# A two-layer mixer stack: square roots behind the last exponentials of differential attention, token differences beside the norm, a rearranged start and moved weight splits

## What is computed

```python
# A two-layer mixer stack: square roots behind the last exponentials of differential attention, token differences beside the norm, a rearranged start and moved weight splits
x = x + rmsnorm(nsa_mixer(rmsnorm(x, norm_pre[0]), ...), norm_post[0])
x = x + rmsnorm(diff_mixer(rmsnorm(x, norm_pre[1]), ...), norm_post[1])
# A two-layer mixer stack: square roots behind the last exponentials of differential attention, token differences beside the norm, a rearranged start and moved weight splits
p = softmax(q @ k.T + bias)                # two maps
o = (p[0] - lam * p[1]) @ v
o = rmsnorm(o, subln) * (1 - lambda_init)  # over the head's 128 columns
y = (o * silu(z)) @ w_out
# A two-layer mixer stack: square roots behind the last exponentials of differential attention, token differences beside the norm, a rearranged start and moved weight splits
xx = shift(u) - u                          # difference to the token before; -u for the first
xw = u + xx * mu[1]                        # and so on for k, v, a, g, r
```

## Time and profile before

| | |
|---|---|
| median of 3 runs | 2272.48 us (2271.74 to 2279.61) |
| the profiled execution, its own time | 2274.92 us |
| its span, first to last instruction | 2273.0 us |
| PE busy | 2070.1 us, 91% |
| DVE, ACT, POOL busy | 848.5, 935.9, 915.2 us |
| mean granted TensorE clock | 0.937 |

### The profile page before, as it was taken

One profiled execution on the slowest core, in us unless ns is written; L12 is line 12 of the kernel. 1 busy time (PEld: TensorE's weight loads), 2 busy tenths in 40 slices (PEclk: granted clock), 3 DMA queues, 4 the chain that ended last, 5 costly groups with the idle time before them and its releaser, 6 DMA issues.

```text
span 2273.0 us, 33586 instructions
## 1 busy us (share of the span) xinstructions
PE 2070.1 (91%) x13582; PEld 1661.5 (73%) x13582; DVE 848.5 (37%) x1813; ACT 935.9 (41%) x1707; POOL 915.2 (40%) x636
## 2 busy tenths in 40 slices
PE   4999999999997968997588899999999899999998
PEld 3889756788765746776477588888878568888886
DVE  2100467340027375146565353333033524334301
ACT  3431477453247354443133353444143535344422
POOL 2431267534446322341012734455434542544542
PEclk9987999999998969898589999999999999999999
DMA  4322100123310211221210323333322121333332
GB/s 119 93 78 65 47 20 2 48 69 101 93 56 19 70 42 49 76 75 38 49 31 19 101 62 98 102 93 111 102 75 84 38 66 56 102 97 98 103 111 74
DMA packets 222361, 161.05 MB, mean 71 GB/s; under 512 B 30631, under 2 KB 205295, under 8 KB 222208
## 3 DMA queue, kind: packets, MB, share of 16 engines
q1 hardware_dynamic: 220016, 151.83, 22.6%
q0 software_dynamic: 2192, 7.07, 1.0%
HBM read 153.64 MB, written 5.24 MB: 70 GB/s over the span
## 4 chain that ended last, share of the span: by engine, by line
PE 79%; DVE 9%; ACT 4%; POOL 3%; issue 3%; DMA 1%; POOLq 1%; SPq 0%; DVEq 0%; PEld 0%; PEldq 0%; ACTq 0%
PE ps L386 15%; PE ps L348 13%; PE ps L350 13%; PE ps L359 13%; PE ps L396 7%; PE ps L1355 2%; PE ps L1368 2%; PE ps L1344 2%; POOL weights_lo L289 1%; DVE ps L901 1%; DVE buffer L906 1%; PE ps L1082 1%; PE ps L2892 1%; PE ps L2156 1%; PE ps L1703 1%
## 5 line engine op out<-in xcount | busy, mean ns | idle before, releaser
L289 POOL TENSOR_TENSOR weights_lo<-buffer,weights_hi 128x1024 fp32r<-128x1024 f32 (+1 forms) x265 | 654.0, 2470 | 981.4 <-ACT weights_hi L278 981.2
L278 ACT ACTIVATE weights_hi<-buffer 128x1024 fp32r<-128x1024 f32 (+1 forms) x265 | 276.4, 1045 | 340.7 <-PE ps L396 285.5
L348 PE MATMUL ps<-u_hi,weights_hi 128*128 128x512 f32 (+1 forms) x752 | 278.5, 378 | 5.6 <-DVE u_lo L681 3.0
L350 PE MATMUL ps<-u_lo,weights_hi 128*128 128x512 f32 (+1 forms) x736 | 274.8, 377 | 0.0
L1931 ACT ACTIVATE buffer<-ps,buffer 128x512 f32<-128x512 f32 x88 | 68.7, 781 | 276.4 <-PE ps L359 276.4
L359 PE MATMUL ps<-u_hi,weights_lo 128*128 128x512 f32 (+1 forms) x752 | 177.2, 378 | 0.0
L1961 DVE SCALAR_TENSOR_TENSOR buffer<-ps,buffer,buffer 128x511 f32<-128x511 f32 x88 | 66.0, 750 | 287.7 <-ACT buffer L1931 287.7
L348 PEld LDWEIGHTS ps<-u_hi,weights_hi 128*128 128x128 f32 x752 | 141.2, 190 | 32.0 <-issue 5.6
L350 PEld LDWEIGHTS ps<-u_lo,weights_hi 128*128 128x128 f32 x736 | 138.4, 188 | 25.5
L359 PEld LDWEIGHTS ps<-u_hi,weights_lo 128*128 128x128 f32 x752 | 137.0, 191 | 25.8
L2932 ACT ACTIVATE buffer<-ps 32x256 f32<-32x256 f32 (+5 forms) x96 | 47.7, 498 | 152.9 <-PE ps L2892 68.1
(11 more groups left out here) (403 smaller groups left out, 4277.5 us busy)
## 6 DMA issues: line engine op xcount, KB each, us to landing
buffer<-in_w_up SPq DMA_DIRECT2D x88, 512.0 KB, 3.8
buffer<-in_w_down SPq DMA_DIRECT2D x44, 512.0 KB, 3.4
buffer<-in_diff_w_in SPq DMA_DIRECT2D x32, 512.0 KB, 4.0
buffer<-in_nsa_w_in SPq DMA_DIRECT2D x28, 512.0 KB, 3.8
buffer<-in_w_rkv SPq DMA_DIRECT2D x24, 512.0 KB, 4.1
buffer<-in_nsa_w_out SPq DMA_DIRECT2D x8, 512.0 KB, 3.5
buffer<-in_diff_w_out SPq DMA_DIRECT2D x8, 512.0 KB, 3.6
buffer<-in_w_o_rwkv SPq DMA_DIRECT2D x8, 512.0 KB, 3.4
```

The costliest lines, as they stand in the source:

```text
L278: self.nc.scalar.activation(self.part_hi[:, part % self.PARTS, 0:n], self.raw[:, ld % self.RAW, 0:n], ACT.Copy).then_inc(self.hi_ready, 1)
L289: self.nc.gpsimd.tensor_tensor(self.part_lo[:, part % self.PARTS, 0:n], self.raw[:, ld % self.RAW, 0:n], self.part_hi[:, part % self.PARTS ...
L348: nc.tensor.matmul(out, hi[:, k, :], rhs[0][:, k, tokens], start=(k == 0), stop=False)
L350: nc.tensor.matmul(out, hi[:, k, :], rhs[1][:, k, tokens], start=False, stop=False)
```

## The change

1. Start: x comes as three transfers; the barriers after `Setup` and `Norm` are gone on all engines; the small vectors and the bias table's source are fetched after the first three weight tiles, and their turns and copies stand in `NsaProject` before the bias table; the norm's scaling is one DVE operation (`Renorm.scale`) instead of one on DVE and one on ACT; ACT loads its Sqrt table first.
2. `DiffAttend`: the first root now covers batches 0 to 5 and stands after the last exponentials, the others one batch each behind it; all norms stand after the last unit, in the order 0, 2, 4, 6, 1, 3, 5, 7; all engines go on to `Output` without a barrier, whose turns wait for the count of norms (`wait_rows`).
3. `Output` before `RwkvProject`: DVE makes the differences by token tile (`difference`) between the steps of the norm, the last one at the head of `RwkvProject`; ACT's order of squares, units, high parts and splits is another.
4. `SwaProject` and `SwaAttend`: of the three splits in the loop, one now stands at the end of the projection, two after the loop.
5. `FfnUp`: both layers share one set of semaphores; the order on each engine is the same. The diff is cut to its added and removed lines; this edit, `Setup`'s memory, and `FfnUp`'s lines are left out.

```diff
@@ -525,8 +527,14 @@
     def load(self, sp):
...
-        sp.dma_start(env.x, io["x"].rearrange("b (t p) d -> p (b t) d", p=P)).then_inc(self.x_arrived, 16)
-        sp.dma_start(env.const, io["shape_constants"]).then_inc(self.const_arrived, 16)
+        for i, end in enumerate((1, 2, NT)):
+            sp.dma_start(env.x[:, i:end, :],
+                         io["x"][0, i * P:end * P, :].rearrange("(t p) d -> p t d", p=P)).then_inc(self.x_arrived[i], 16)
+            if i == 0:
+                sp.dma_start(env.const, io["shape_constants"]).then_inc(self.const_arrived, 16)
...
+    def load_vectors(self, sp):
+        io = self.env.io
@@ -549,23 +557,23 @@
-    def tensor(self, pe):
+    def vectors_tensor(self, pe):
...
-        pe.wait_ge(self.const_arrived, 16)
-        pe.wait_ge(self.tab_arrived, 64)
...
-            tr = nc.tensor.transpose(env.ps[:, n // 4, (n % 4) * P:(n % 4) * P + size], self.rows[0:size, n, :],
+            tr = nc.tensor.transpose(env.ps[:, 6 + n // 4, (n % 4) * P:(n % 4) * P + size], self.rows[0:size, n, :],
...
     def bias_tensor(self, pe):
...
+        pe.wait_ge(self.tab_arrived, 64)
+        pe.wait_ge(self.table_ready, 1)
...
-            if i >= 4:
-                pe.wait_ge(self.bias_taken, i - 3)
+            if i >= 2:
+                pe.wait_ge(self.bias_taken, max(i - 2, 1))
@@ -573,12 +581,14 @@
     def vector(self, dve, step):
-        env, nc = self.env, self.env.nc
-        nc.vector.memset(env.eps, EPS)
+        nc = self.env.nc
+        nc.vector.memset(self.env.eps, EPS)
...
+    def table_vector(self, dve, step):
+        nc = self.env.nc
@@ -643,6 +657,14 @@
+    def scale(self, dve, i):
...
+        env, nc = self.env, self.env.nc
+        dve.wait_ge(env.next_g_arrived, 16 * self.g_n)
+        dve.wait_ge(env.rstd_ready, self.n + i + 1)
+        nc.vector.scalar_tensor_tensor(self.un[:, i, :], env.x[:, i, :], self.rstd[:, i:i + 1], env.next_g,
+                                       ALU.mult, ALU.mult).then_inc(env.un_ready, 1)
...
     def invert(self, dve, i):
@@ -694,31 +716,44 @@
-    def __init__(self, env, g_row, u, x_arrived):
+    def __init__(self, env, g_row, u, setup):
...
-        self.norm, self.x_arrived = Renorm(env, g_row, u), x_arrived
+        self.norm, self.setup = Renorm(env, g_row, u), setup
+        self.tensor_goes_on = self.scalar_goes_on = self.vector_goes_on = self.gpsimd_goes_on = True
     def gpsimd(self, pool, step):
...
     def scalar(self, act, step):
-        act.wait_ge(self.x_arrived, 16)
-        for i in range(NT):
-            self.norm.square(act, step, i)
-            self.norm.unit(act, i)
-        self.env.split_hi(act, 1)
-        for i in range(NT):
-            self.norm.high(act, i)
+        env, norm = self.env, self.norm
+        act.wait_ge(self.setup.rows_zeroed, 1)
+        env.nc.scalar.activation(env.sqrt_junk, env.eps, ACT.Sqrt)
...
+        def square(i):
+            act.wait_ge(self.setup.x_arrived[min(i, 2)], 16)
+            norm.square(act, step, i)
...
+        for i in range(3):
+            square(i)
+        norm.high(act, 0)
+        square(3)
+        norm.high(act, 1)
+        env.split_hi(act, 0)
+        norm.high(act, 2)
+        norm.high(act, 3)
+        env.split_hi(act, 1)
     def vector(self, dve, step):
...
-            self.norm.gain(dve, i)
...
-        for i in range(NT):
-            self.norm.low(dve, i)
+            self.norm.scale(dve, i)
+            if i:
+                self.norm.low(dve, i - 1)
+        self.norm.low(dve, NT - 1)
     def tensor(self, pe):
+        pe.wait_ge(self.setup.const_arrived, 16)
@@ -768,6 +804,8 @@
+        if self.rows:
+            self.rows.wait_rows(pe, k)
@@ -842,7 +880,17 @@
-        if self.norm:
+        if self.norm and self.shifted:
+            square_x(2)
+            self.norm.high(act, 1)
+            self.norm.unit(act, 2)
+            square_x(3)
+            env.split_hi(act, self.lds[-1] + 1)
+            self.norm.unit(act, 3)
+            self.norm.high(act, 2)
+            env.split_hi(act, self.lds[-1] + 2)
+            self.norm.high(act, 3)
+        elif self.norm:
@@ -901,6 +949,8 @@
+                if self.shifted:
+                    self.norm.invert(dve, 2)
@@ -912,12 +962,17 @@
-                self.norm.invert(dve, i - 1)
+                if not self.shifted or i < NT - 1:
+                    self.norm.invert(dve, i - 1)
...
+                if i >= 2 and self.shifted:
+                    self.shifted.difference(dve, self.norm, i - 2)
...
+            if self.shifted:
+                self.shifted.difference(dve, self.norm, 2)
@@ -953,9 +1008,10 @@
+        self.setup.vectors_tensor(pe)
...
-        pe.wait_ge(self.setup.bias_taken, 8)
+        pe.wait_ge(self.setup.bias_taken, 9)
@@ -964,6 +1020,8 @@
     def vector(self, dve, step):
+        self.setup.table_vector(dve, step)
+        self.setup.vectors_vector(dve, step)
...
     def gpsimd(self, pool, step):
@@ -1677,10 +1735,12 @@
-    LOTS = [(0, 5), (5, 8)]
+    LOTS = [(0, 6), (6, 7), (7, 8)]
+    NORMS = [0, 2, 4, 6, 1, 3, 5, 7]
     def __init__(self, env, m):
@@ -1688,7 +1748,15 @@
+        self.normed = s("diff_normed")
+        self.tensor_goes_on = self.scalar_goes_on = self.vector_goes_on = self.gpsimd_goes_on = True
...
+    def wait_rows(self, pe, k):
...
+        if k < 2:
+            pe.wait_ge(self.o_taken, 7 + k)
+        pe.wait_ge(self.normed, 4 if k < 4 else 8)
     def slot(self, u):
@@ -1779,10 +1847,11 @@
-            if u == 26:
+            if u == n_units:
...
+        root(1)
...
-        root(1)
+        root(2)
     def four(self, b):
@@ -1831,9 +1900,10 @@
         def norm(b):
-            dve.wait_ge(self.rms_ready, 1 if b < self.LOTS[0][1] else 2)
+            dve.wait_ge(self.rms_ready, 1 + max(b - 5, 0))
...
-            nc.vector.tensor_tensor(o, o, m.nrstd[:, b, :].unsqueeze(2).to_broadcast([P, 4, P]), ALU.mult)
+            nc.vector.tensor_tensor(o, o, m.nrstd[:, b, :].unsqueeze(2).to_broadcast([P, 4, P]),
+                                    ALU.mult).then_inc(self.normed, 1)
@@ -1844,11 +1914,13 @@
-            if 28 <= u < 33:
-                norm(u - 28)
+            if u > n_units:
+                norm(self.NORMS[u - n_units - 1])
+        norm(4)
...
+        norm(6)
...
-        for b in range(*self.LOTS[1]):
+        for b in self.NORMS[4:]:
...
     def gpsimd(self, pool, step):
@@ -2062,7 +2131,7 @@
     def gpsimd(self, pool, step):
...
-        self.env.split_lo(pool, self.q[-1][0])
+        self.env.split_lo(pool, self.q[-1][0] + 1)
     def tensor(self, pe):
@@ -2078,7 +2147,7 @@
-            env.split_hi(act, min(ld + 1, self.q[-1][0]))
+            env.split_hi(act, min(ld + 1, self.q[-1][0]) + (j >= KD - 2))
@@ -2203,8 +2271,6 @@
-            if u in self.SPLITS:
-                env.split_hi(act, self.ahead - 2 + self.SPLITS.index(u))
@@ -2214,6 +2280,7 @@
+        env.split_hi(act, self.ahead)
     def gpsimd(self, pool, step):
@@ -2235,12 +2302,11 @@
-            if u in self.SPLITS:
-                self.env.split_lo(pool, self.ahead - 2 + self.SPLITS.index(u))
...
+        self.env.split_lo(pool, self.ahead)
     def vector(self, dve, step):
@@ -2481,10 +2547,19 @@
+    def difference(self, dve, norm, i):
...
+        env, xx = self.env, self.m.xx
+        dve.wait_ge(env.uT_ready, norm.n + i + 1)
+        if i == 0:
+            env.nc.vector.tensor_scalar(xx[:, :, 0:1], env.uT[:, :, 0:1], -1.0, None, ALU.mult)
+        t0, t1 = max(i * P, 1), (i + 1) * P
+        return env.nc.vector.tensor_tensor(xx[:, :, t0:t1], env.uT[:, :, t0 - 1:t1 - 1], env.uT[:, :, t0:t1], ALU.subtract)
...
     def vector(self, dve, step):
...
-        step(v.tensor_scalar(m.xx[:, :, 0:1], env.uT[:, :, 0:1], -1.0, None, ALU.mult))
+        step(self.difference(dve, self.norm, NT - 1))
         def mix(n, k):
@@ -2503,8 +2578,6 @@
-                if n == 0:
-                    step(v.tensor_tensor(m.xx[:, k, 1:T], env.uT[:, k, 0:T - 1], env.uT[:, k, 1:T], ALU.subtract))
@@ -3254,6 +3329,8 @@
+                if ld == env.RAW - 1:
+                    setup.load_vectors(sp)
```

49 lines of the change are left out of this document (26 added, 23 removed).

## The result

| | before | after |
|---|---|---|
| median | 2273.86 us (2271.74 to 2279.61, 4 runs) | 2236.80 us (2234.47 to 2244.81, 4 runs) |
| ratio after to before | | 0.9834, 95% interval 0.9808 to 0.9861 |
| profiled execution, its own time | 2274.92 us | 2244.81 us, the slowest of the four |
| TensorE busy, granted clock | 2070.1 us, 0.937 | 2074.1 us, 0.936 |

1.66% less, 37.7 us (31.6 to 43.7). The forecast was 2233.5 us, range 2222 to 2246, "faster" with 0.95: right in sign, and 3.3 us off the median. The profiled execution was the slowest of its four.

What follows compares the result with a forecast made beforehand. TensorE is 79% of the chain of waits, so time is won only where it stands still for another engine. 16.1 (start less bias table) + 3.5 + 5.6 + 14 = 39.2 us, predicting 2233.5 us, range 2222 to 2246.

Steps and rivals of the forecast that it cites:

- Start: Up to the first projection: its first matmul moves from 39.64 to 21.5 us, 18.1 us won, bounds 15 and 21.
- I give them 1.3: Start: low parts of 1.15 us each queued on VectorE before tile 3's scaling were charged 1.3 us.
- taken as 1.23: Start: the one-pass scaling of tile 3 on VectorE was assumed to take 1.23 us.
- rival (a): Start: transfers don't come earlier because x shares with the weights, x 3.6 us later; total 2239 us; chance 0.10.
- Bias table: Between first projections and bias table: moved vector turns and copies cost 2.0 us, bounds nothing and 3.1.
- Differential roots: End of differential attention to output: table-load stall and barrier go, 3.5 us won, bounds 2.0 and 6.5.
- Token differences: RWKV mixing: 4.3 us from a shorter first pass, 1.3 from the earlier last high part; 5.6 won, bounds 3.5 and 6.5.
- Sliding window: Sliding-window loop: without splits pairs take 1.65 us, 16 us less by calculation, taken as 14; bounds 7.0, 12.2 and 16.
- rival (b): Sliding-window loop is slower by itself, only the low parts' own time goes: 7 instead of 14 us, 2240.5; chance 0.11.
- rival (c): Sliding-window output: late splits come too late, TensorE waits 5.6 us for them; total 2239 us; chance 0.04.
- (d): Whole kernel: effect hidden within 0.5%, because remaining VectorE and GpSimd waits fill every gap; chance 0.03.
- Rival (e): First projections: TensorE stays at its lower clock after the earlier start, adding 53 us: 2286.5, 0.6% slower; chance 0.02.

Runs made afterwards that it cites:

- v_order: Changed kernel, but ScalarE squares all four tiles before the first high part and VectorE scales all four before the first low part; 2237.33 us, 0.9833 of before.
- p_swa: Kernel before with only the three weight splits moved out of the sliding-window attention loop; ratio to before 0.9910, 20.5 us less.
- v_late: Changed kernel, but SP asks for the projection's weights only when the last piece of x has landed; 2233.06 us, 0.9815 of before.
- v_barrier: Changed kernel, but ScalarE and VectorE go on from the differential output into the RWKV mixing without the barrier; 2234.58 us, 0.9819 of before.
- v_diff: Changed kernel with the differential attention's two weight splits moved out of its loop, one to the projection before, one behind the loop; 2235.48 us, 0.9842 of before.

## Why the forecast was right, term by term

- **Start, 18.1 us: 13.7** in the first profile, 14.4 to 14.8 by the others of this start. The size was off, just beyond its bound of 15. The step that failed is "I give them 1.3": tile 3's root was ready at 16.13 and its scaling began at 18.80, behind low parts and reciprocals on VectorE, which is 1.2 us more than the step had. The one-pass scaling "taken as 1.23" took 2.71 beside GpSimd, 1.4 more. Turn, high and low part took 0.4 more. With the four squares and scalings ahead of the low parts, v_order won 4.4 us, both causes at once. The last piece of x came at 12.39 and not 10.8 (11.23 to 11.67 in the others); the weights of rival (a) explain some 0.5 us of this, if anything.
- **Bias table, 2.0: 0.8.** The copies run at 1.04 us for six, not the 1.67 of the start, where each waited for the one before. All copies took 8.3 us (93.73 to 102.04) where the forecast wanted 10.5.
- **Differential roots, 3.5: 3.6 to 3.7** up to the first product, and 1.4 in the output stage that the step did not have; 5.7 (3.4 to 8.0) timed alone. The mechanism is the one named: measured from the first scores, the last exponential ends 2.9 us earlier and the first product starts 3.6 us earlier.
- **Token differences, 5.6: 4.8** at the place, 3.6 (1.4 to 5.7) timed. Of the two terms, the one for the mixing pass (4.3) gave 2.8: the step not seen is GpSimd's weight split as the last at the barrier, 1.5 us. The one for the earlier last high part (1.3) gave 2.0.
- **Sliding window, 14: 16.2 in the loop, 19.0 with what follows in p_swa.** The 16 of the bare calculation was right, rounding it down was not; rival (b) with 7 is refused, and so is rival (c): TensorE is busy 10.00 of the output's first 10 us. What the step did not name is the clock: 6.0 of the 16.2 us come with a granted clock of 1.00 instead of 0.87.
- **The sum, 39.2: 37.7 (31.6 to 43.7).** It is near by luck, through offsetting errors: 3 us too much at the start with its bias table, 2 to 5 too little in the sliding window, and a loss that nobody forecast, 4.3 us between mix_k and mix_v. Rivals (a), (b) and (c), at 2239 to 2240.5 us, lie inside the interval: it is the traces that refuse them, not the time. Rivals (d) and (e) lie outside it. Rival (e)'s argument had one slip: the first seven matmuls of the projection stand 0.43 us apart, in both kernels, and only then 0.23; the 1.00 of the earlier trace rows hides this, and it cost the same before and after.

## What to carry over

Before moving work to an engine that idles, look what its neighbour does at that time: three splits moved out of the sliding-window loop paid 5.4 us each, and one moved from the differential loop to a tail of VectorE operations paid nothing. When a queue holds short urgent and long patient work, put all the urgent work first; here that was worth 4.4 us, far more than the order of the transfers. Judge a part by how stretches between landmarks shorten, not by one profiled total. But have a second profile of the same kernel at hand: between executions of the same code the core differed by 4.8 us, an earlier stage by 4.2, and the arrival of x by 1.1, and v_late's 1.5 us look like an effect only until they are held against that last spread.

## What the runs showed of the hardware

**VectorE behind GpSimd.** In four places an operation of VectorE with all tensors in SBUF waited out GpSimd's low part of a weight tile. The scaling took 2.71 instead of 1.28 us (after, and again in v_late), the difference 2.33 instead of 1.22, two mixes 3.37 instead of 1.42, four norms 4.61 instead of 2.46. Each time VectorE ends about as if it had only begun when GpSimd was done: in v_barrier GpSimd ends at 789.20, and 1.22 later would be 790.42; the operation ended at 790.28. The low parts L703, whose one input lies in PSUM, are not delayed: four take 4.61 us with GpSimd's operation beside them (v_order), 4.62 before. GpSimd is held up too: in v_diff a norm was already running when it began, and it took 2.71 instead of 2.36. The Trainium skill has this as a rule (SBUF — State Buffer, section SBUF: two separate sides): a VectorE operation with two SBUF inputs and a GpSimd operation that reads SBUF share a port pair as an exclusive lock, and whichever starts first keeps it for its whole instruction. The trace agrees in all four places.

**The clock.** TensorE's granted clock made the same 3156 matmuls of the core last 204.5 to 210.6 us without any change that touches them. And from the first differential scores to the first mix_v matmul, 4 to 5 us of what the roots and the differences win alone are missing in all nine kernels that hold both. In the changed kernel they are busy time of the same matmuls and not standing still, and the stretch from mix_k to mix_v has a granted clock of 0.89 there and 0.93 or 0.94 with either part alone.

**Table loads.** A table load took 1.28 us on ScalarE and nothing more: in the differential loop before, the operation behind it starts 1.29 to 1.30 us after the load did (721.51 and 723.04).
